# Two attention heads on the column halves of TensorE, and a new order around them, in a two-block transformer kernel

## The reference

```python
def chunked_relbias_attention(q, k, v, rel_bias):        # branch A: 8 heads of 64
    scores = jnp.einsum("bcqhd,bckhd->bchqk", qc, k_band) / math.sqrt(d)
    scores = jnp.where(valid, scores + bias[None, None], NEG_INF)
    probs = jax.nn.softmax(scores, axis=-1)
    return jnp.einsum("bchqk,bckhd->bcqhd", probs, v_band).reshape(b, s, h * d)

def differential_attention(q, k, v, lam, ...):           # branch B: 4 heads of 128, two softmaxes each
    w = softmax(s1) - lam * softmax(s2)
    out = w @ v                                          # then an RMS norm per head
...
merged = g_a * (o_a @ w_branch_a) + g_b * (o_b @ w_branch_b)      # g: sigmoid gates of x
x = layer_norm(alpha * x + merged @ w_out)
h = square(relu(x @ w_ff1))
x = layer_norm(alpha * x + h @ w_ff2)
```

## Time and profile before

| | us |
|---|---|
| three runs | 2250.28, 2250.88, 2254.11 (median 2250.88) |
| the profiled execution | 2253.48 |
| its span | 2251.7 |
| TensorE busy | 2206.9 (98%) |
| VectorE busy | 1687.7 (75%) |
| ScalarE busy | 1243.1 (55%) |
| POOL busy | 568.7 (25%) |
| TensorE's mean granted clock | 0.995 of full |

### The profile page before, as it was taken

How to read it: one execution, slowest core, us unless ns; L and a number is a source line. 1 busy time by engine, 2 the same in 40 slices (tenths; PEclk the granted TensorE clock), 3 DMA queues, 4 the chain that set the end, 5 groups by cost and what they waited for, 6 DMA issues and landing times.

```text
span 2251.7 us, 29477 instructions
## 1 busy us (share of the span) xinstructions
PE 2206.9 (98%) x10718; PEld 1811.7 (80%) x10718; DVE 1687.7 (75%) x1616; ACT 1243.1 (55%) x1285; POOL 568.7 (25%) x399
## 2 busy tenths in 40 slices
PE   8999999999999999999999999989999999999998
PEld 6778878888888888888888888877777878888886
DVE  7577699998999999999999999982567446423334
ACT  5246267776787777877768777742444522422320
POOL 4170169982232322322223222200220010000000
PEclk9999999999999999999999999999999999999999
DMA  5230279999999999999999999943221332323221
GB/s 194 67 124 25 87 279 390 398 387 376 391 382 400 378 391 386 381 400 376 393 384 384 397 379 389 362 159 111 60 80 38 120 123 94 112 76 111 99 88 38
DMA packets 142081, 552.29 MB, mean 245 GB/s; under 512 B 11712, under 2 KB 12864, under 8 KB 124976
## 3 DMA queue, kind: packets, MB, share of 16 engines
q1 hardware_dynamic: 128928, 507.95, 58.4%
q0 software_dynamic: 10592, 38.41, 6.6%
q10 hardware_dynamic: 2480, 4.80, 0.6%
HBM read 522.66 MB, written 25.69 MB: 244 GB/s over the span
## 4 chain that ended last, share of the span: by engine, by line
PE 84%; DVE 8%; POOL 4%; ACT 1%; issue 1%; DMA 1%; DVEq 0%; SPq 0%; POOLq 0%; ACTq 0%
PE PS L428 79%; DVE low L2319 3%; PE PS L811 1%; PE PS L760 1%; ACT act L1981 1%; POOL act L3019 1%; POOL xs L3003 1%; DVE st L2071 1%; DMA ring<-w_down 1%; DVE small L2691 1%; POOL xs L2998 1%; PE PS L637 0%; DMA acc_d<-act,to_c 0%; DVE act L2103 0%; DVE ring_parts L2596 0%
## 5 line engine op out<-in xcount | busy, mean ns | idle before, releaser
L428 PE MATMUL PS<-act_parts 128*128 128x512 f32 (+2 forms) x3392 | 1052.9, 398 | 2.1 <-DVE xs L2475 1.5
L2319 DVE TENSOR_TENSOR low<-ring,act_parts 128x2048 fp32r<-128x2048 f32 x380 | 859.9, 2316 | 32.6 <-ACT act_parts L1719 32.5
L428 PEld LDWEIGHTS PS<-act_parts 128*128 128x128 f32 (+2 forms) x3392 | 619.1, 188 | 143.0 <-issue 9.5
L1719 ACT ACTIVATE act_parts<-ring 128x2048 fp32r<-128x2048 f32 x384 | 706.8, 1911 | 12.0 <-PE PS L428 9.2
L428 PE MATMUL PS<-low,act_parts 128*128 128x512 f32 x1584 | 618.3, 390 | 0.0
L428 PE MATMUL PS<-act_parts,ring_parts 128*128 128x512 f32 (+3 forms) x1696 | 466.5, 374 | 0.0
L428 PEld LDWEIGHTS PS<-act_parts,ring_parts 128*128 128x128 f32 (+1 forms) x1696 | 302.3, 187 | 67.5 <-issue 13.3
L428 PEld LDWEIGHTS PS<-low,act_parts 128*128 128x128 f32 x1584 | 298.3, 188 | 58.8
L428 PE MATMUL PS<-ring_parts,act_parts 128*128 128x512 f32 (+2 forms) x1208 | 272.9, 383 | 3.1 <-DVE act_parts L2768 2.1
L428 PEld LDWEIGHTS PS<-ring_parts,act_parts 128*128 128x128 f32 (+1 forms) x1208 | 219.7, 188 | 50.2 <-issue 3.9
L428 PE MATMUL PS<-ring_parts 128*128 128x512 f32 (+1 forms) x672 | 250.8, 380 | 0.0
(11 more groups left out here) (305 smaller groups left out, 1905.6 us busy)
## 6 DMA issues: line engine op xcount, KB each, us to landing
ring<-w_gate_up SPq DMA_DIRECT2D x264, 1024.0 KB, 8.5
ring<-w_down SPq DMA_DIRECT2D x132, 1024.0 KB, 7.9
ring<-w_ff SPq DMA_DIRECT2D x16, 2048.0 KB, 7.7
ring<-w_in SPq DMA_DIRECT2D x12, 2048.0 KB, 9.8
ring<-w_o SPq DMA_DIRECT2D x1, 4096.0 KB, 14.6
ring<-w_out SPq DMA_DIRECT2D x2, 2048.0 KB, 7.8
acc_d<-ring POOLq DMA_DIRECT2D x5, 512.0 KB, 6.5
act<-x SPq DMA_DIRECT2D x4, 512.0 KB, 5.6
```

The lines of the kernel that those rows point to most:

```text
L428: return eng.matmul(o, lhsT, rhs, start=first, stop=last, **kw)
L1719: A_(W1hi[c % CS], W1[c], ACT.Copy).then_inc(sem["high"], 1)
L2319: tt(W1lo[c], W1[c], W1hi[c % CS].bitcast(F32), ALU.subtract).then_inc(sem["low"], 1)
```

## The change

1. `attend_a` swaps its sides: a head's values (64 columns) are the weights, the turned probabilities (128 columns) move, and the two heads of a pair write to partitions 0 to 63 and 64 to 127 of one bank. The result is turned already, so branch A has no `turn_heads`. The probabilities are normed by VectorE before they are turned (`normed_a`), and `out_a` is one plain copy into `OA`.
2. The heads of A are split one group of 128 rows at a time inside branch B (`heads_a_high`, `heads_a_low`, at the units of `HEADS_AT`).
3. `scores_b(0)` with its piece goes ahead of `turn_a(15)`, `attend_a(15)` one unit back to u = 1; the banks of B go on from 5.
4. The last two sines go one unit forward, and the pieces of slots 5 and 6 too.
5. In VectorE's units of B the split piece stands between `masked` and `mix_b`.
6. Blocks 0 and 1 of branch 0 (banks 6 and 7) go into the two closing units of B.
7. In the last half of the feed-forward the last two chunks go by tile, and the statistics of a tile's first half are taken at once.

```diff
-ROPE_AT = (6, 7, 8, 9, 12, 13, 14, 15)
+ROPE_AT = (6, 7, 8, 9, 12, 13, 13, 14)
-SPLIT_A = ((4, 0), (5, 6), (6, 11))
+SPLIT_A = ((4, 0), (5, 5), (6, 10))
+HEADS_AT = (4, 5, 6, 12)
...
             def turn_a(q):
                 for e in range(2):
-                    eng.wait_ge(*past("proba", 2 * q + e + 1))
+                    eng.wait_ge(*past("inva", 2 * q + e + 1))
...
-                for e in range(2):
-                    h = 2 * pair + e
-                    for j in range(t + 1):
-                        ins = mm(PS[:, 4, e * DH:(e + 1) * DH], p4[:, e, j * P:(j + 1) * P],
-                                 va2[:, j, h * DH:(h + 1) * DH], j == 0, j == t)
-                    ins.then_inc(put("oa_psum", 4), 1)
+                for j in range(t + 1):
+                    for e in range(2):
+                        h = 2 * pair + e
+                        ins = mm(PS[e * DH:(e + 1) * DH, 4, 0:P], va2[:, j, h * DH:(h + 1) * DH],
+                                 p4[:, e, j * P:(j + 1) * P], j == 0, j == t)
+                ins.then_inc(put("oa_psum", 4), 1)
...
+            def branch_block(br_, f, b):
+                eng.wait_ge(*free[b])
+                free[b] = past(f"branch{br_}_out", f + 1)
+                product(b, slot2_parts(8 + 3 * br_), block_of(f), (o2hi[br_], o2lo[br_]), ALL, 4).then_inc(
+                    put(f"branch{br_}_psum", b), 1)
...
-            eng.wait_ge(*past("rope2_done", 8))
+            for q in range(UA + 1):
+                if q < UA:
+                    scores_a(q)
+                    for n in beside_a(q):
+                        beside(n)
+                else:
+                    eng.wait_ge(*past("rope2_done", 8))
+                    cur[0] = 0
+                    scores_b(0)
+                    beside(24)
+                if 1 <= q <= UA:
+                    turn_a(q - 1)
+                if 2 <= q <= UA:
+                    attend_a(q - 2)
             for u in range(UB + 2):
-                if u < UB:
+                if 1 <= u < UB:
                     scores_b(u)
                     beside(24 + u)
-                if u == 0:
+                if u == UB:
+                    slot(8)
+                    eng.wait_ge(*past("o2T_lo", NT))
+                if u >= UB:
+                    branch_block(0, u - UB, 6 + u - UB)
+                if u == 1:
                     attend_a(UA - 1)
-                if u == UB:
-                    turn_heads(0)
+                    cur[0] = 5
...
+                if br_ == 0:
+                    cur[0] = 0
+                for f in range(0 if br_ else 2, KD):
+                    branch_block(br_, f, next_bank())
                     if br_ == 0 and f == 3:
-                        turn_heads(1)
+                        turn_heads()
...
+                w = slot(28)
+                for t in range(2):
+                    out_chunk(w, 2, t)
+                last = slot(29)
+                for t in range(2):
+                    out_chunk(last, 3, t)
+                for t in range(2, NT):
+                    for hf in range(2):
+                        out_chunk(w, 2, t, (hf,))
+                        out_chunk(last, 3, t, (hf,))
...
-                for e in range(2):
-                    h, c = 2 * pair + e, 8 + 2 * (q % 2) + e
-                    A_(XN[:, t, h * DH:(h + 1) * DH], bank_of("oa_psum", 2 * q + 1)[:, e * DH:(e + 1) * DH], ACT.Copy,
-                       scale=small[:, c:c + 1]).then_inc(signal("oa_out"), 1)
+                A_(OA[:, pair, t * P:(t + 1) * P], bank_of("oa_psum", q + 1)[:, 0:P], ACT.Copy).then_inc(
+                    signal("oa_out"), 1)
...
+            def heads_a_high(k):
+                A_(o2hi[0][:, k, :], OA[:, k, :], ACT.Copy).then_inc(signal("o2T_hi"), 1)
...
-                if u == 0:
+                if u == 1:
                     out_a(UA - 1)
-                if u == UB:
-                    heads_high(0)
+                    eng.wait_ge(*past("oa_out", UA))
+                if u in HEADS_AT:
+                    heads_a_high(HEADS_AT.index(u))
...
+            def normed_a(q):
+
+                n, c = (q % NT + 1) * P, 2 * (q % 2)
+                eng.wait_ge(*past("proba", 2 * q + 2))
+                eng.reciprocal(small[:, 8 + c:10 + c], small[:, 4 + c:6 + c]).then_inc(signal("dve_step"), 1)
+                eng.wait_ge(*latest("dve_step"))
+                for e in range(2):
+                    p = e4[:, q % 2, e, 0:n]
+                    ts(p, p, small[:, 8 + c + e:9 + c + e], None, ALU.mult).then_inc(signal("inva"), 1)
...
                 if q:
                     take_a(q - 1)
+                if q < UA:
+                    normed_a(q)
...
                     masked(u)
-                    mix_b(u)
-                if u == UB:
-                    heads_low(0, range(2))
-                if 1 <= u <= UB:
-                    take_b(u - 1)
+                if u - 1 in HEADS_AT:
+                    heads_a_low(HEADS_AT.index(u - 1))
                 for n, at in SPLIT_B:
                     if at < u <= at + PIECES:
                         split_piece(n, u - at - 1)
-                if u == UB:
-                    heads_low(0, range(2, NT))
+                if u < UB:
+                    mix_b(u)
+                if 1 <= u <= UB:
+                    take_b(u - 1)
...
+                    if half and hf == 0:
+                        half_stats(XN, t, 0)
                     if half and hf:
-                        eng.wait_ge(*past("ff_out", 8 + n + 1))
-                        stats(XN, 4, t)
+                        stats(XN, 4, t, halves=(1,))
```

More of the change, by code:

```diff
@@ L335, in build @@
         X2lo = ring_parts[:, (NW + NH) * SW:].rearrange("p (k s) -> p k s", k=KD)
[L336 to L337 removed]
+        OA = XN[:, :, 0:512]
+        o2hi = [part(12288, 4, S), part(16384, 4, S)]
+        o2lo = [part(0, NT, D)[:, :, 0:512], part(20480, 4, S)]
         G2 = v(8192, KD, S)
@@ L1156, in _ @@
                 eng.wait_ge(*past(f"{name}_out", 4))
-            for q in range(UA + 1):
-                if q < UA:
-                    scores_a(q)
-                    for n in beside_a(q):
-                        beside(n)
-                if 1 <= q <= UA:
-                    turn_a(q - 1)
-                if 2 <= q <= UA:
-                    attend_a(q - 2)
             def scores_b(u):
@@ L1235, in _ @@
                         product(b, w, block_of(f), X2, ALL, KD).then_inc(put("gate1_psum", b), 1)
-                eng.wait_ge(*past("o2T_lo", NT * (br_ + 1)))
-                w = slot(8 + 3 * br_)
-                for f in range(KD):
-                    b = next_bank()
-                    eng.wait_ge(*free[b])
-                    free[b] = past(f"branch{br_}_out", f + 1)
-                    product(b, w, block_of(f), (o2hi[br_], o2lo[br_]), ALL, 4).then_inc(
-                        put(f"branch{br_}_psum", b), 1)
+                if br_:
+                    eng.wait_ge(*past("o2T_lo", 2 * NT))
+                    slot(11)
+                if br_ == 0:
+                    cur[0] = 0
+                for f in range(0 if br_ else 2, KD):
+                    branch_block(br_, f, next_bank())
                     if br_ == 0 and f == 3:
-                        turn_heads(1)
+                        turn_heads()
             def mix_product(hf, t, b, w, piece):
@@ L1934, in out_a @@
                 pair, t = q // NT, q % NT
-                eng.wait_ge(*past("inva", q + 1))
-                eng.wait_ge(*past("oa_psum", 2 * q + 2))
+                eng.wait_ge(*past("oa_psum", q + 1))
                 if q == 0:
```

103 lines of the change are left out of this document (54 added, 49 removed).

## The result

The changed kernel takes 2238.6 us, the median of six runs (2236.97 to 2242.29), beside 2250.86 for the kernel before on the same chip (2250.28 to 2254.25): a ratio of 0.9944, with a 95% interval of 0.9934 to 0.9953. A second set of five runs, on another chip, gave 2236.99 against 2252.06, 0.9936 [0.9922, 0.9949]. The forecast was 2238.6.

A forecast was written before the change was run, and what follows sets the result against it. TensorE bounds the kernel (84% of the last-ending chain). Gains 6.6 + 1.0 - 0.4 + 0.4 + 1.1 + 1.8 + 1.8 = 12.3 us take the profiled 2253.5 to 2241.2; the median, 2.6 lower before, gives 2238.6, range 2234.0 to 2248.5.

The forecast's parts named there:

- The column halves: Branch A's attends: two heads on different column halves overlap as on row halves, so the attends gain 6.6 us.
- rival 1: Branch A's attends: the column halves run one after the other, losing 2.8 us instead of gaining 6.6; 2248.0 us, chance 0.15.
- Rival 3: Branch A's attends: every step from one column half to the other empties the array; slower, 2262.8 us, chance 0.06.
- Rival 4: Branch A's attends: column halves aren't formed and the pace stays 0.115 us; 2245.2 us, chance 0.05.
- Waits of A: Branch A: the 1.0 us wait for slot 5 goes, while later exponentials make unit 9's scores 0.4 late.
- Rival 2: Branch A's norming: POOL holds VectorE, 0.5 us at each of eight rotations; +4, 2242.6 us, chance 0.08.
- The seam: From branch A to B: waits of 1.2 and 0.48 us go, a copy wait of 1.3 comes; net gain 0.4.
- Branch B: VectorE's split piece fills its idle hole before the mixing, so TensorE's two waits on the mixing go: 1.1 us gained.
- Slot 9: End of branch B, before the gate products: TensorE waits 2.9 us anew for the split of this weight slot.
- The clock: Behind the new wait before the gate products the clock may fall, costing 1.4 us, or 0 if it doesn't.
- The tail: Last feed-forward blocks by tile, half the last tile's sum and statistics done ahead: VectorE ends 1.8 us earlier.
- the end of B: From the first turned heads to the gate products: reordered blocks and fewer transposes gain 1.8 us, up to 3.2.

## Why the prediction was right, and where it was off

**The column halves.** That they overlap like the row halves was right: one half alone takes 1.89 where both take 1.03, and rival 1 would have cost 8.6 us. Rival 3, an emptied array at each alternation, falls with the same rows: 0.22 for a pair of heads and a block of keys, though the heads alternate at every block. Rival 4 (1.84) falls too. The term was mis-sized in its parts: the groups gained 7.3 (18.5 to 11.2) instead of 6.6, but the transposes ahead of all but the first and the last pay 0.10 each, 1.4 together (8.8 to 10.2). Net 5.9. I had put the change of shape inside the attend group, at the 0.21 of the scores, where a part of it was in the old groups already (their last instruction took 0.205 to the scores, the others 0.112, so 0.09); the part on the way into the column halves falls on the group in front, and I had not costed it. The runs price a step between shapes of the array at 0.08 to 0.10 in front of it and 0.05 to 0.06 behind column halves.

**Waits of A.** The 1.0 on slot 5 went, and 0.4 at unit 9 came as forecast (0.41 at 1613.52). The 1.1 at unit 15 wasn't forecast. Rival 2 named its mechanism, VectorE held by POOL, but gave it 0.5 us at each of eight rotations; it reached TensorE at one, and in half of the eight traces with the same code there.

**The seam.** A copy's wait of 1.4 came where 1.3 was forecast, the net was 0.3 of 0.4. Not seen was how much the moved sines carry: 4.2 of wait and 1.7 of clock.

**Branch B.** -2.5 instead of -1.1. The two waits on L2710 were only the listed part. Every fourth unit took 4.77, 5.30 and 5.43 us where it now takes 4.5. The wait in the second of them, before:

```profile
1709.74 0.39 PE L428 MATMUL PS<-act_parts,ring_parts 128*128 128x512 f32 x1
1710.62 0.66 PE L1185 MATMUL PS<-cm,act 128*128 128x128 f32 x4 [0.49 <-DVE act L2710]
```

and the same place after:

```profile
1701.63 0.39 PE L430 MATMUL PS<-act_parts,ring_parts 128*128 128x512 f32 x1
1701.86 0.60 PE L1181 MATMUL PS<-cm,act 128*128 128x128 f32 x4
```

The list counts 0.49 from the modelled end of the last product; from start to start it is 0.88 instead of 0.23, so 0.65 lost, and the two groups behind lose 0.13 more. In the first of the three units the wait is so short that the list leaves it out. The step that failed is that the sum went by the list and not by the starts of the units.

**Slot 9.** A wait of 2.4 where 2.9 was forecast, on the split as named. Its chain, ScalarE's part:

```profile
1745.92 5.02 ACT L2055 ACTIVATE act<-act,bgc 128x512 f32<-128x512 f32 x8
...
1754.52 3.67 ACT L1908 ACTIVATE ring_parts<-ring 128x4096 fp32r<-128x4096 f32 x1
```

and VectorE's:

```profile
1758.29 4.43 DVE L2622 TENSOR_TENSOR ring_parts<-ring,ring_parts 128x4096 fp32r<-128x4096 f32 x1 [1.98 <-ACT ring_parts L1908]
```

It is the chain of the earlier trace rows with the same durations. The stage gained 3.6 against 3.2.

**The clock.** In the changed kernel's first trace the granted clock fell behind that wait, as forecast. The row is its 4 us from 1764 on, with the granted clock last but two, 0.57:

```profile
1764.00:1768.00 4.00, 4.00 (x12) 3.10 (x11) 4.00 (x3) 0.15 (x1) 0.00 (x0) 0.57 1.02 419
```

The same 4 us of its second trace, behind the same wait of 2.4:

```profile
1764.00:1768.00 4.00, 4.00 (x20) 3.30 (x19) 4.00 (x2) 0.10 (x1) 0.00 (x0) 1.00 1.03 423
```

The fall (to 0.50 in the two microseconds from 1765 on) costs 4 x 0.43 = 1.7, against 1.4 forecast, and stands in five of the ten traces that have the wait. Before the change the clock also fell at 1844 to 1848, behind the waits ahead of `w_out`, for 1.7; these waits are as long after (1.5 and 0.7), and in none of the twelve traces since has it fallen there. So the term of 1.4 was right in size, and a toss in its coming; in the first pair of traces it is cancelled by a fall that I hadn't counted at all.

**The tail.** 1.7 against 1.8, shown by undoing it.

**The sum.** Against the forecast, A with its waits and the seam gained 2.0 less, the tail 0.1 less, B 1.4 more, the end of B 0.4 more; and the clock cost the changed trace 0.3 on balance where 1.4 was forecast, since one fall came and another went. So the profiled executions lie 13.2 apart from A's first scores on, not 12.3, and another 2.0 lie ahead of them, where nothing changed. The medians lie 12.3 apart: the profiled run of before stood 2.6 above its median and held two clock falls, 3.4 us, so it was probably a dear one (the other runs of before kept no trace), and by its own time the forecast of 2241.2 for the profiled run was 2.8 too high.

## What to carry to other kernels

The matmuls of two heads, 128 columns each, overlapped fully on different column halves when they alternated (sixteen instructions in 1.03 us against 1.89 on one half); count the steps between shapes of the array as well, here about 0.1 us in the group in front and 0.06 in the one behind column halves. When TensorE's work shrinks or moves forward, price what else must come sooner at its new place, not by the old wait: the sines were worth 0.5 by the old trace and 5.8 by the new ones. Read small waits from the starts of repeated units, and look at a second trace before a wait of one operation's length is put down to the change.

## What was not expected of the hardware

- Two heads of four instructions each overlap on column halves even one after the other (0.59), eight each only in part (1.51 against 1.03 in turn and 1.89 on one half).
- The same wait of 2.4 us was followed by a granted clock of 0.50 in five traces and of 1.00 in five.
- The same two operations of VectorE and POOL, with the same 0.37 between their starts, take 2.32 and 1.61 us or 1.22 and 2.73, and only the first costs TensorE anything (1.1 us).
